# A merge moved ahead of split work on VectorE, scalings moved between ScalarE's high parts, conditioning rows moved into a norm

## The reference

```python
mod = silu(c) @ w_ada + b_ada                 # sh1, sc1, g1, sh2, sc2, g2
h = layer_norm(x) * (1 + sc1) + sh1
a_val, a_gate, u_pool, gate_a, gate_b = split(h @ w_in)
ya = causal_dwconv(a_val * sigmoid(a_gate), w_dw_a, b_dw_a)   # 31 taps, 512 channels
ya = silu(layer_norm(ya, ln_a_g, ln_a_b)) @ w_pw_a
yb = pooled_means(u_pool) @ w_pool * pool_scale
merged = sigmoid(gate_a) * ya + sigmoid(gate_b) * yb
x = layer_norm(ALPHA * x + g1 * (merged @ w_out), ln1_g, ln1_b)
h = layer_norm(x) * (1 + sc2) + sh2
up = causal_dwconv(h @ w_up, w_dw_f, b_dw_f)                  # 3 taps
x = layer_norm(ALPHA * x + g2 * ((gelu(gt) * v) @ w_down), ln2_g, ln2_b)
```

## Time and profile before

| | |
|---|---|
| median of 3 runs | 1143.19 us (1142.56 to 1143.68) |
| profiled execution | 1137.92 us, its span 1136.0 us |
| TensorE busy | 1082.1 us, 95% of the span |
| VectorE busy | 794.0 us, 70% |
| ScalarE busy | 596.2 us, 52% |
| low parts, line 1668 | 311, mean 1221 ns |
| high parts, line 1138 | 311, mean 1051 ns |
| conditioning rows, line 1655 | 48, mean 1218 ns |
| mean granted TensorE clock | 0.983 |

### The profile page before, as it was taken

The page is one execution under the profiler, slowest core; times in us unless marked ns, Lnnn a source line. Parts: engine busy times, 40 slices in busy tenths (PEclk is TensorE's granted clock), DMA queues, the critical chain, the costliest instruction groups (busy, mean ns, idle before and its releaser), DMA issues.

```text
span 1136.0 us, 19220 instructions
## 1 busy us (share of the span) xinstructions
PE 1082.1 (95%) x7892; PEld 1018.4 (90%) x7892; DVE 794.0 (70%) x1374; ACT 596.2 (52%) x1003; POOL 3.3 (0%) x13
## 2 busy tenths in 40 slices
PE   7998999999999999879989999999999899999997
PEld 7998889899999998779988799999899788999996
DVE  7988789878877788586755745555688747455555
ACT  5567543565465557633444644445565546454453
POOL 0000000000000000000000000000000000000000
PEclk9999989999999999989989999999999999999999
DMA  9985257357766613233222545566455235555520
GB/s 375 418 336 181 93 181 264 113 190 241 244 209 213 191 70 130 85 89 125 93 75 93 184 154 189 180 194 194 149 202 169 93 116 210 175 187 187 190 69 38
DMA packets 58550, 195.57 MB, mean 172 GB/s; under 512 B 10848, under 2 KB 11232, under 8 KB 58208
## 3 DMA queue, kind: packets, MB, share of 16 engines
q1 hardware_dynamic: 58464, 194.35, 49.9%
HBM read 193.01 MB, written 1.31 MB: 171 GB/s over the span
## 4 chain that ended last, share of the span: by engine, by line
PE 75%; DVE 16%; ACT 6%; issue 2%; SPq 1%; DMA 0%; POOL 0%; ACTq 0%; DVEq 0%; POOLq 0%
PE ps L543 63%; DVE lo L1668 4%; PE ps L835 3%; ACT hi L1138 2%; DVE raw L1655 2%; PE ps L718 1%; PE ps L648 1%; DVE B L2071 1%; DVE ev L1907 1%; PE ps L538 1%; DVE ev L1904 1%; DVE B L1677 1%; PE ps L550 1%; PE ps L841 1%; DVE B L1783 1%
## 5 line engine op out<-in xcount | busy, mean ns | idle before, releaser
L1668 DVE TENSOR_TENSOR lo<-raw,hi 128x1024 fp32r<-128x1024 f32 x311 | 377.0, 1221 | 161.8 <-ACT hi L1138 161.0
L543 PE MATMUL ps<-hh,hi 128*128 128x256 f32 x1568 | 447.4, 285 | 12.0 <-DVE hl L1760 3.1
L543 PE MATMUL ps<-hl,hi 128*128 128x256 f32 x1568 | 441.8, 282 | 0.0
L543 PE MATMUL ps<-hh,lo 128*128 128x256 f32 x1568 | 441.7, 282 | 0.0
L1138 ACT ACTIVATE hi<-raw 128x1024 fp32r<-128x1024 f32 x311 | 322.9, 1051 | 57.6 <-PE ps L543 57.6
L543 PEld LDWEIGHTS ps<-hh,hi 128*128 128x128 f32 x1568 | 299.0, 191 | 17.0 <-issue 7.3
L543 PEld LDWEIGHTS ps<-hl,hi 128*128 128x128 f32 x1568 | 298.9, 191 | 1.6
L543 PEld LDWEIGHTS ps<-hh,lo 128*128 128x128 f32 x1568 | 298.8, 191 | 0.0
L1374 ACT ACTIVATE ev<-ps 128x256 f32<-128x256 f32 x72 | 27.6, 384 | 109.9 <-PE ps L543 109.9
L543 PE MATMUL ps<-hi,fh 128*128 128x512 f32 x192 | 76.3, 398 | 0.0
L543 PE MATMUL ps<-lo,fh 128*128 128x512 f32 x192 | 75.9, 395 | 0.0
(11 more groups left out here) (278 smaller groups left out, 1317.0 us busy)
## 6 DMA issues: line engine op xcount, KB each, us to landing
raw<-in_w SPq DMA_DIRECT2D x359, 512.0 KB, 4.2
B<-in_t SPq DMA_DIRECT2D x2, 512.0 KB, 4.5
xa<-in_x SPq DMA_DIRECT2D x1, 1024.0 KB, 10.3
B<-in_r SPq DMA_DIRECT2D x1, 1024.0 KB, 6.6
out<-h SPq DMA_DIRECT2D x4, 256.0 KB, 2.0
cst<-in_c SPq DMA_DIRECT2D x1, 928.0 KB, 8.7
B<-between SPq DMA_DIRECT2D x32, 4.0 KB, 1.6
vec<-in_v SPq DMA_DIRECT2D x1, 328.5 KB, 6.3
```

Source lines behind the costliest of these rows:

```text
L543: m = g.matmul(o, l, r, start=first and n == 0, stop=last and n == 2, skip_group_check=True)
L1668: g.tensor_tensor(lo[:, j % SPLIT, :], raw[:, PLACE[j] % RAW, :], hi[:, j % SPLIT, :].bitcast(F), ALU.subtract).then_inc(*up("lo", j))
```

## The change

1. In the plan, three more rows (24 is there already, 25 to 27 are new) stand directly behind `pw` 3, and one row each behind `out` 0 to 5. Before there was one row each behind `pw` 3, `out` 0 to 7 and `up` 0. All units from `up` 22 on keep their positions.
2. The three new rows (positions 58 to 60) are worked off: one ahead of the statistics of the convolution's norm, two behind its coefficients. `LATE` becomes a table that says how many rows `low(j)` takes.
3. The low part of `out` 3, with the row behind it, moves from ahead of the merge to behind the merge's block 4.
4. ScalarE scales x one block at a time, each behind a high part, instead of all eight ahead of them.
5. Of the six late rows, the fourth moves from behind the centring of `h2` to ahead of it.

The number of instructions is the same on every engine.

```diff
--- before.py
+++ after.py
@@ -112,8 +112,11 @@
         if i < 16 and i % 2 == 0:
             plan += [("ada", i // 2), ("ada", 8 + i // 2)]
         plan.append(u)
-        if 20 <= i < 28 or 32 <= i < 42 or (i >= 52 and i % 3 == 0 and rows):
+        if 20 <= i < 28 or 32 <= i < 39 or (i >= 52 and i % 3 == 0 and rows):
             plan.append(rows.pop(0))
+        if i == w.index(("pw", 3)):
+            plan += rows[:3]
+            del rows[:3]
         if i == w.index(("out", 7)) + 4:
             plan += rows[:6]
             del rows[:6]
@@ -130,7 +133,8 @@
 AHEAD = SPLIT - 1
 
 BY_TOKENS = ("x3", "x4", "x5")
-LATE = UNIT["out", 7] + AHEAD
+
+LATE = {UNIT["pw", 3]: 1, UNIT["out", 7] + AHEAD: 0}
 
 
 class Ring:
@@ -1272,9 +1276,8 @@
                 g.activation(hh[:, n, :], mg[:, n, :], ACT.Copy).then_inc(*up("merged_hi", n))
             s.wait_ge(*x_in)
             for k in range(8):
+                high(UNIT["out", k] + AHEAD)
                 scale_x(k)
-            for k in range(8):
-                high(UNIT["out", k] + AHEAD)
 
 
             table(ACT.Sqrt)
@@ -1668,7 +1671,7 @@
                     g.tensor_tensor(lo[:, j % SPLIT, :], raw[:, PLACE[j] % RAW, :], hi[:, j % SPLIT, :].bitcast(F),
                                     ALU.subtract).then_inc(*up("lo", j))
                     for i in range(PLACE[j] + 1, PLACE[j + 1] if j + 1 < len(UNITS) else len(PLAN)):
-                        if j > 15 and j != LATE:
+                        if j > 15 and i - PLACE[j] <= LATE.get(j, 9):
                             ada(i)
 
             def center(nid, y, nch, sq, yc, bm):
@@ -1837,6 +1840,8 @@
             g.tensor_tensor(yb[:, 7, :], yb[:, 7, :], ev[:, 3, :], ALU.mult).then_inc(*up("ybg", 7))
 
 
+            late = PLACE[UNIT["pw", 3]] + 2
+            ada(late)
             for c in range(2):
                 s.wait_ge(*at("ya_tok", c))
                 g.bn_stats(fst[:, c, 0:6], bank[c][:, :]).then_inc(*up("tbn", ("ya", c)))
@@ -1852,13 +1857,15 @@
                 else:
                     g.scalar_tensor_tensor(out=fnm[:, 1, :], in0=fmv[:, 1, 0:1], scalar=-1.0, in1=frs[:, 1, :], op0=ALU.mult,
                                            op1=ALU.mult).then_inc(*up("tnm", ("ya", 1)))
+            ada(late + 1)
+            ada(late + 2)
             for k in range(4):
                 s.wait_ge(*at("silu_y", k))
                 s.wait_ge(*at("unit", UNIT["in", 27]))
                 g.tensor_copy(yh[:, k, :], cv[:, k, :]).then_inc(*up("silu_hi", k))
                 s.wait_ge(*at("silu_hi", k))
                 g.tensor_tensor(yl[:, k, :], cv[:, k, :], yh[:, k, :].bitcast(F), ALU.subtract).then_inc(*up("silu_lo", k))
-            for k in range(4):
+            for k in range(3):
                 low(UNIT["pw", k] + AHEAD)
 
             def merged_low(n):
@@ -1873,22 +1880,25 @@
                 g.tensor_tensor(mg[:, n, :], mg[:, n, :], yb[:, n, :], ALU.add).then_inc(*up("merged", n))
                 if n:
                     merged_low(n - 1)
+                if n == 4:
+                    low(UNIT["pw", 3] + AHEAD)
             merged_low(7)
             for k in range(8):
                 low(UNIT["out", k] + AHEAD)
 
 
             residual_gated("x1", 6, ("out", 7), modcol("g1"), "g1", 0)
-            late = PLACE[LATE] + 1
+            late = PLACE[UNIT["out", 7] + AHEAD] + 1
             ada(late)
             center("x1", xa, 8, B[0], B[1], 4)
             ada(late + 1)
             ada(late + 2)
             root("x1")
             norm_out("x1", 8, B[1], veccol("ln1_g"), veccol("ln1_b"), xa)
+            ada(late + 3)
             center("h2", xa, 8, B[0], B[1], 4)
-            for i in range(3, 6):
-                ada(late + i)
+            ada(late + 4)
+            ada(late + 5)
             root("h2")
             norm_parts("h2", B[1], modcol("sc2"), modcol("sh2"), h, [at("mod", "sc2"), at("mod", "sh2")])
```

## The result

| | before | changed |
|---|---|---|
| first comparison, median | 1142.88 us (1142.54 to 1143.68, 4 runs) | 1134.80 us (1130.88 to 1136.34, 4 runs) |
| ratio of times, 95% interval | | 0.9923 (0.9897 to 0.9950) |
| second comparison, median | 1140.16 us (1135.82 to 1144.54, 16 runs) | 1132.88 us (1129.68 to 1135.16, 6 runs) |
| ratio of times, 95% interval | | 0.9935 (0.9915 to 0.9955) |
| profiled execution (its span) | 1137.92 us (1136.0) | 1130.88 us (1128.8) |

The change makes the kernel faster by 7 to 8 us. The gain that was forecast, 6.7 us, lies in both intervals (5.7 to 11.8 us and 5.1 to 9.7 us).

The account below looks back on a forecast made before the run. Before the residual, VectorE's run and TensorE's `out` rows were taken to bound the kernel together. 5.5 us there and 1.14 at the second centring make 6.7; 1143.19 - 6.7 = 1136.5 us, range 1134.0 to 1140.2.

Parts of the forecast that it names:

- Both must get shorter: Before the residual: VectorE's run from 165.12 and TensorE's `out` rows end together, so a gain needs both shortened.
- Part 1: Three rows in VectorE's holes of 1.84 and 2.70 us in the convolution's norm: no cost; uncovered, 3.4 us.
- The rival that held each row for twice its length: Rows in the norm overrun the two holes by 2.4 us; gain 4.3 us, time 1138.8; chance 0.02.
- the estimate of 2.2 us per row: Rows in the norm: pipe emptying makes each 2.2 us, two 4.3 in a 2.70 us hole; time 1138.4.
- Part 2: Merge ahead of the fourth split: `out` starts at 152.27, 2.67 us earlier; no slow stretch, 2.7 us less on TensorE.
- Part 3: Scalings between ScalarE's high parts: TensorE stalls 0.2 us, residual starts at 174.6 instead of 180.14, term 5.5 us.
- Part 4: One row ahead of the second centring, in a 1.42 us idle: second reciprocal 1.14 us earlier.
- The sum: Whole change: 5.5 + 1.14 = 6.7 us gained, carried over to the median 1143.19 to give 1136.5.
- the last one, that the rest shifts as a whole: First feed-forward network behind the change: same instructions and order, transfers freed no later, so it shifts as a whole.
- rival B: Merge not early, or rows in the norm late: time 1138.8 to 1142; chance 0.07.
- rival C: Clock falls in more places, 2.7 us per stretch; from the third on slower, time 1144.6; chance 0.03.
- A: Clock still falls in the `out` rows: `out` 6 ends 2.7 us later, gain 4.0, time 1139.2; chance 0.10.

Follow-up runs that it names:

- 1: Kernel before with 22 filler matmuls on TensorE between the `pw` and the `out` rows; ratio 1.0015 (1.0002 to 1.0027), slower by 1.7 us.
- 9: Kernel before with only the fourth split and its row moved behind the merge's block 4; ratio 0.9999 (0.9988 to 1.0010).
- 2: Changed kernel with the fourth split and its row back ahead of the merge; ratio 0.9956 (0.9936 to 0.9975) against the kernel before.
- 3: Changed kernel with all eight scalings of x back ahead of the next high parts; ratio 0.9969 (0.9954 to 0.9984) against the kernel before.
- 4: Changed kernel with the old plan, no rows in the convolution's norm; ratio 0.9982 (0.9966 to 0.9999) against the kernel before.
- 10: Kernel before with only the three rows moved into the convolution's norm; ratio 0.9985 (0.9971 to 0.9998).
- 11: Kernel before with only the scalings of x put between the high parts; ratio 0.9973 (0.9960 to 0.9985).
- 5: Changed kernel run again, unchanged, in more runs; ratio 0.9935 (0.9915 to 0.9955) against the kernel before.
- 6: Changed kernel with the fourth late row back behind the second centring; ratio 0.9957 (0.9942 to 0.9972) against the kernel before.

## Why the prediction was right

**What bounds the kernel.** Right that VectorE's run set the residual: filling TensorE's hole gained nothing there (1), and starting TensorE early gained 0.43 us (9). Once all of the change is in, each of its three large parts is worth 2.5 us or more when it is taken out (2 to 4). "Both must get shorter" was too strong: with the clock up behind the hole, the rows or the scalings alone, which relieve only VectorE, brought 2.5 and 2.4 of the 5.4 us (10, 11). Only the rest needs TensorE shorter as well. With a slow stretch behind the hole, as in the profile that the prediction read, the two parts alone were never seen, so for that case the sentence stays untested.

**Part 1, the rows in the norm.** Right to 0.2 us in each place. They cost nothing there, and the residual is 2.5 us earlier for them (4). They take 3.4 us off VectorE's run, but its last split then waits 0.82 us for ScalarE. The rival that held each row for twice its length falls: the two rows in the second hole start 1.14 us apart. So does the estimate of 2.2 us per row that I had worked out from the Trainium skill, "VectorE: DVE Perf Modes", section "The DRAIN you can't avoid": that is not what these rows show. The same section adds "A next op that is not held starts earlier", which I had left out; the 1.14 us between two rows of 1.22 us agree with that sentence.

**Part 2.** The merge's head start was put at 2.67 us and measured 2.73, TensorE's start at 152.27 and measured 152.12. The slow stretch is gone. What I held for a consequence of the hole is none that its length alone decides: 3.01 and 3.03 us of idle were followed by no slow stretch in 2 and 10. For the kernel before, the forecast did not hang on it, because VectorE's run bounded it either way. For the changed kernel it did need the full clock in the `out` rows, and both its profiles have that.

**Part 3.** Right: without it TensorE waits 2.50 us (3), I had 2.3. The residual came at 174.62. The reason why the scalings fit was right only in part. I had ScalarE waiting 1.7 us for TensorE before each high part there; in the changed kernel it waits before the last two (0.70 and 1.43 us). The first six run with their scalings and no pause, about 1.26 us apart, and they cost nothing because ScalarE still stays ahead of VectorE, which waits only for the first and the last high part.

**Part 4.** 1.14 us forecast, 1.15 measured.

**The sum.** 6.7 us forecast to the feed-forward network, 6.6 found from the statistics on. The profiled executions differ by 7.0 (1137.92 to 1130.88). The assumption that failed by a little is the last one, that the rest shifts as a whole: it is 0.55 us shorter. Two slips of the prediction have no weight: rival B's gain of 4.3 us gives 1138.9 and not 1138.8, and rival C's "6.7 - 8.1 = +1.4" is a loss of 1.4. The median of the first comparison is 1.7 us below the point. The four executions of the changed kernel in that comparison show how much of that the clock may be:

| time | span | mean granted clock |
|---|---|---|
| 1130.88 | 1128.8 | 0.986 |
| 1134.05 | 1132.2 | 0.984 |
| 1135.56 | 1133.1 | 0.981 |
| 1136.34 | 1134.3 | 0.981 |

The same instructions take 5.5 us longer where the mean clock is 0.005 lower. The kernel before spreads in the same way: of its 35 runs in the comparison with experiments 1 to 4 the fastest took 1135.36 us at 0.987, and one of the slowest 1142.96 us at 0.978. Its profiled execution (0.983) was one of the faster, and the 5.3 us to its first median have the size of this spread; the clocks of those first runs are not recorded, so that part stays open.

**The rivals.** A (the clock still falls in `out`) did not happen in either profile of the changed kernel, but its neighbour did, a slow stretch in `pw` (5). B did not happen. C named the right mechanism in the wrong kernel: with TensorE's hole filled alone the clock fell elsewhere and the kernel became slower (1), and the same cost 1.7 us in 4. The whole change has no such pause: TensorE starts its last `out` matmul at 174.81 and the norm's sums at 175.15. The slow stretch in `pw` cost 1.5 us, less than the 2.7 that C reckoned for one.

## What to carry to other kernels

Where two engines reach a common point at nearly the same time, shortening the one that is not last gives nothing, and can cost: TensorE was early, paused, and its clock fell in the next stage, where it was the bound. Shortening the one that is last gives only the distance to the next bound, here 2.5 of 5.4 us. Count the queue of each engine to the next common point, and move work until all of them get shorter. Small independent operations (here the rows) belong in holes that end with another engine's work; check that hole minus work stays positive, and what is late next.

## What the runs showed of the hardware

Neither the kernel nor the length of a pause tells whether TensorE's clock falls. It fell to 1.2 GHz behind 2.32 us of idle (9), 2.50 (3), 2.70 (1), 2.81 (4) and 2.83 (the kernel before), and it stayed at 2.4 GHz behind 2.83 (11), 3.01 (2) and 3.03 us (10). Each of these is one execution of another kernel. In one and the same kernel, the changed one, it fell in the `pw` rows in one of two profiles. What decides it stays open. A slow stretch cost 1.4 to 1.7 us in experiments 1, 3, 4 and 5, where it lay on the path, and nothing in 9, where it lay beside VectorE's run. So a difference of under 2 us between two single profiles of this kernel says nothing until the slow stretches are counted in both. The distances between two marks without a slow stretch between them repeat much better: from the statistics to the residual 40.61 us in two kernels whose work there is the same (the changed one and 6).
